# A gated delta-rule mixer: triangular inverses in three stages of two levels, and products of raw q and k

## The chip, the cores and the metric

One core of a Trainium2 chip runs the whole kernel. The metric is the device time in microseconds (us) of one execution; the times below are of three runs. Engines: PE is TensorE's matmul stream, PEld its weight loads, DVE is VectorE, ACT is ScalarE, POOL is GpSimd, SP is SyncE, which issues the DMAs.

## The reference

One step of a decoder layer for a prompt of 16 + 1024 tokens and 8 samples of 8 tokens: feed-forward, a mixer with two branches, feed-forward, final norm. The change lies in branch B, the gated delta rule over 8 heads of width 128:

```python
def l2norm(x):
    return x * lax.rsqrt(jnp.sum(x * x, axis=-1, keepdims=True) + L2_EPS)
...
    q = l2norm(q) * (GDN_DK ** -0.5)
    k = l2norm(k)
    beta = jax.nn.sigmoid(b_raw)
...
    a_kk = beta[..., :, None] * jnp.einsum('bnhid,bnhjd->bnhij', k, k) * dec_strict
    rhs = jnp.concatenate([beta[..., None] * v, (beta * jnp.exp(g))[..., None] * k], axis=-1)
    sol = lax.linalg.triangular_solve(a_kk, rhs, left_side=True, lower=True, unit_diagonal=True)
    u, w = sol[..., :dv], sol[..., dv:]
    a_qk = jnp.einsum('bnhid,bnhjd->bnhij', q, k) * dec_incl
...
        nu = u_c - w_c @ s
        o = qd_c @ s + aqk_c @ nu
        s = exp(gl_c) * s + kd_c.T @ nu
...
    o = rmsnorm(o, norm_g) * jax.nn.silu(zh)
```

## The kernel before

All tokens are one row of 1104 columns, features on the partitions. The kernel runs in stages: turning the inputs, feed-forward 1, the mixer (from about 860 to 2310 us), the merge of the branches, feed-forward 2, the output. In float32 the large products are made of three passes over a high and a low part of each operand (`three_passes`, L209 to L211), each a matmul with 368 moving columns.

The mixer first projects q, k and v for eight heads, with a short convolution on VectorE (`head_conv`, L1897). Then come 16 full **turns** and two odd ones for the last 80 tokens. A turn u handles 128 tokens of four heads (group g = u mod 2) and carries, as filler on TensorE, 36 pieces of dense projections (z, the gates, branch A), six matmuls each. `turn_order` (L884) writes one list of steps, and every engine walks that list in order, doing its part of each step; a step in `NEXT_STEPS` (L939) is done for the turn that follows. Two turns make one pass of a hardware loop.

The steps of a turn: `kk` and `qk` (products of k with k and with q), `kt` (transposes of k and v to tokens on the partitions; L1523, L1526), `zero` (T0 transposes the first level of the masked matrix, L1529, and starts the inverse). Then the inverse of the 128 x 128 unit triangle is doubled in six levels: `Y` (L1533) multiplies the masked level with the transposed inverse, ScalarE copies it, `X` (L1543) multiplies that with the half of the inverse's columns that changes, VectorE subtracts (L1888), `T` (L1537) transposes the result, ScalarE copies it (L1736). Between them: `ks` (L1568, k with the state), and for the next turn the sums `dec`, `eg`, `sq`, `sk` (all L1503, 512 columns wide), where sq and sk sum the squares of q and k, from which ScalarE makes the norms by Ln and Exp (L1723, L1727) and VectorE scales q and k in place (`scale`, L1865, L1868). At the end `nu`, `o` and `ds` (L1548, L1574, L1580), `os` (L1552: sum of the squares of the output), and `out` (Ln, Exp and the scaled output; L1739, L1741, L1894). `evict` empties a projection's bank: VectorE first, and in group-1 turns ScalarE with Silu or Sigmoid (L1780). `split` makes the high and low parts of the next weight (L812 on ScalarE, L817 on GpSimd). `conv` is a step of branch A's convolution on VectorE. GpSimd masks levels (L1386), the decay and others. SP loads q, k and v of the next turn at the start of a turn, in group-0 turns only after the y and gate stores of the turn before.

Turn 0 is prepared in the last pass of `head_conv`: four sums on TensorE between projections (L1654), and the scaling of q and k at j = 2 (L1918).

Of the kernel before, what the change touches and what calls it, by code (L numbers as in the profile page):

```python
# [36 lines left out]
EPS = 1e-6  # L37
SC_T = 3
# [790 lines left out]
class Events:  # L829


    def __init__(self, s, label):
# [14 lines left out]
        self.rooted = s.sem(label + "rooted")  # L847
        self.y_ready = s.sem(label + "y_ready")
# [3 lines left out]
class HeadGroup:  # L852
# [31 lines left out]
def turn_order():  # L884
# [17 lines left out]
    order.append(("lu", 0))  # L902
    dense(1)
    order.append(("qk", 0))
    order.append(("kt", 0))
    dense(1)
    order.append(("zero", 0))
    order.append(("square", 0))
    dense(2)
    for k in range(1, LEVELS):  # L910
        order.append(("Y", k))
        if k == 1:
            order.append(("ks", 0))
# [12 lines left out]
        dense(1 if k > 4 else 2)  # L926
# [12 lines left out]
NEXT_STEPS = ("load", "lu", "square", "dec", "eg", "sq", "sk", "mask", "scale")  # L939
# [84 lines left out]
for _name, _width in (("upto", P), ("upto_tail", TAIL), ("after", P), ("after_tail", TAIL), ("level", LEVELS * P),  # L1024
# [6 lines left out]
def delta_constants():  # L1031
# [7 lines left out]
    def put(name, a):  # L1039
# [7 lines left out]
                                 for k in range(LEVELS)], 1))  # L1047
# [4 lines left out]
def mixer(nc, base, h_hi, h_lo, slots, ahead, w_a, raw_at, x_at, x, rstd, gains, ones, ident, eps_col, w_in, sc_taps, gc_taps, sc_hist, gc_hist, sc_tail, gc_tail,  # L1052
# [8 lines left out]
    with ExitStack() as ctx:  # L1061
# [50 lines left out]
        state = m.sb("state", [P, H, P])  # L1112

# [7 lines left out]
        N = Units(s, "n", [(name, 0) for name in ("dec", "eg", "sq", "sk")], [n_bank])  # L1121
        names = ["kk", "qk", "kt", "vt", "T0"]
        for k in range(1, LEVELS):
            names += [f"Y{k}"] + (["ks"] if k == 1 else []) + [f"X{k}"] + ([f"T{k}"] if k < LEVELS - 1 else [])
# [27 lines left out]
        full = [HeadGroup(P, g, LEVELS, N, A, full_on) for g in range(2)]  # L1152
        for g, d in enumerate(full):
            d.q, d.k, d.v, d.eg = q[g], k_n[g], v[g], eg[g]
            d.qk_loaded, d.v_loaded = s.sem(f"qk_loaded{g}"), s.sem(f"v_loaded{g}")
            d.sq, d.lu, d.dec, d.bdec, d.bmat, d.bk, d.aqk, d.w_inv, d.y_lev = sq, lu, dec, bdec, bmat, bk, aqk, w_inv, y_lev
            d.kdec, d.resid, d.x_inv, d.nu, d.o, d.o_sq = kdec, v_tok, x_inv, nu, o, o_sq
            d.upto, d.after = const("upto"), const("after")
# [7 lines left out]
        tails = [HeadGroup(TAIL, g, TAIL_LEVELS, N, O, full_on) for g in range(2)]  # L1166
# [7 lines left out]
        for g, d in enumerate(tails):  # L1174
# [3 lines left out]
            d.sq, d.bk = odd_view(sq[:, :, :, :], P, 2, HG, TAIL), odd_view(bk[:, :, :, :], TAIL, 2, HG, TAIL)  # L1178
# [197 lines left out]
        def _(pool):  # L1376
# [1090 lines left out]
```

## Time and profile before

| | |
|---|---|
| median of three runs | 3411.95 us |
| lowest and highest | 3410.54 and 3413.16 us |
| the profiled execution | 3409.4 us |
| its span, first to last instruction | 3407.6 us |
| PE busy | 3300.6 us, 97% |
| VectorE, ScalarE, GpSimd busy | 39%, 30%, 26% |
| granted clock of TensorE, mean over the span | 0.983 |
| first to last full turn's start | 1162.45 to 2107.20 us |

How to read it: engines run beside each other, so shares don't add up. A busy PE is not PE at its peak, as matmuls are pipelined and each lasts longer than the distance to the next; what a matmul costs is read start to start in the timeline. A line of waits names what an engine sat idle for, and what ended the idle time.

### The profile page before, as it was taken

To read this page: it belongs to the slowest core of one execution; us is meant where nothing else is said; L and a number is where in the kernel's file an instruction comes from. 1 tells how busy PE (TensorE), PEld (TensorE's weight loads), DVE (VectorE), ACT (ScalarE), POOL (GpSimd) and SP (SyncE) were. 2 spreads that over 40 slices of the span, in tenths; PEclk is the share of its full clock that TensorE was granted. 3 is DMA by queue.
4 is the path that set the end of the run, shared out by engine and by line. 5 is a ranking of instruction groups with operands and counts; after the bars stand their busy time and mean duration, and the time that the engine had idled before them with its cause. 6 is when DMAs were issued, how large, how long until landed. Compare 5 with 4: busy or idle time off the path is not lost. (4 is left out here: it accounts for less than half of the span.)

```text
span 3407.6 us, 51601 instructions
## 1 busy us (share of the span) xinstructions
PE 3300.6 (97%) x20286; PEld 3228.4 (95%) x20286; DVE 1343.8 (39%) x2193; ACT 1018.3 (30%) x1412; POOL 891.1 (26%) x506
## 2 busy tenths in 40 slices
PE   8999999998999999999999999898999999999998
PEld 8999999998999899999999999878999999999997
DVE  4333333334677633333333333344224333333333
ACT  5111111113322354554544544412123111111113
POOL 2121111123222333333323323221143122211212
PEclk9999999999999999999999999898999999999998
DMA  4111111112233212212112112438212111111101
GB/s 134 44 41 48 46 44 43 37 39 72 70 95 100 87 52 63 65 52 70 59 51 68 57 51 72 141 105 291 78 41 72 38 49 43 43 43 43 40 28 53
DMA packets 275570, 227.04 MB, mean 67 GB/s; under 512 B 12170, under 2 KB 251914, under 8 KB 275440
## 3 DMA queue, kind: packets, MB, share of 16 engines
q1 hardware_dynamic: 275140, 225.08, 21.8%
q8 instruction: 84, 1.38, 0.2%
q10 hardware_dynamic: 324, 0.41, 0.0%
q14 instruction: 22, 0.18, 0.0%
HBM read 172.92 MB, written 52.54 MB: 66 GB/s over the span
## 5 line engine op out<-in xcount | busy, mean ns | idle before, releaser
L209 PE MATMUL ffn_bank<-ffn_h_hi,ffn_w_hi 128*128 128x368 f32 x2112 | 698.1, 331 | 6.8 <-DVE ffn_h_lo L618 6.8
L210 PE MATMUL ffn_bank<-ffn_h_lo,ffn_w_hi 128*128 128x368 f32 x2112 | 699.0, 331 | 0.0
L211 PE MATMUL ffn_bank<-ffn_h_hi,ffn_w_lo 128*128 128x368 f32 x2112 | 697.7, 330 | 0.0
L209 PE MATMUL mix_bank<-both_h_hi,mix_w_hi 128*128 128x368 f32 x1848 | 676.7, 366 | 10.8 <-issue 5.9
L408 POOL TENSOR_TENSOR ffn_w_lo<-g_w_raw,ffn_w_hi 128x1024 fp32r<-128x1024 f32 x130 | 310.9, 2401 | 1191.7 <-ACT ffn_w_hi L404 1191.6
L210 PE MATMUL mix_bank<-both_h_lo,mix_w_hi 128*128 128x368 f32 x1848 | 613.1, 332 | 0.0
L211 PE MATMUL mix_bank<-both_h_hi,mix_w_lo 128*128 128x368 f32 x1848 | 611.9, 331 | 0.0
L817 POOL TENSOR_TENSOR mix_w_lo<-g_w_raw,mix_w_hi 128x1024 fp32r<-128x1024 f32 x77 | 196.4, 2551 | 837.2 <-ACT mix_w_hi L812 837.2
L209 PEld LDWEIGHTS ffn_bank<-ffn_h_hi,ffn_w_hi 128*128 128x128 f32 x2112 | 398.2, 189 | 8.1 <-issue 8.0
L211 PEld LDWEIGHTS ffn_bank<-ffn_h_hi,ffn_w_lo 128*128 128x128 f32 x2112 | 398.0, 188 | 0.0
L210 PEld LDWEIGHTS ffn_bank<-ffn_h_lo,ffn_w_hi 128*128 128x128 f32 x2112 | 397.7, 188 | 0.1
L209 PEld LDWEIGHTS mix_bank<-both_h_hi,mix_w_hi 128*128 128x128 f32 x1848 | 351.5, 190 | 34.6 <-issue 26.1
L645 DVE SCALAR_TENSOR_TENSOR g_x<-ffn_bank,g_x 128x368 f32<-128x368 f32 x528 | 284.1, 541 | 225.7 <-PE ffn_bank L211 225.4
L210 PEld LDWEIGHTS mix_bank<-both_h_lo,mix_w_hi 128*128 128x128 f32 x1848 | 351.5, 190 | 20.8 <-issue 19.1
L211 PEld LDWEIGHTS mix_bank<-both_h_hi,mix_w_lo 128*128 128x128 f32 x1848 | 350.2, 189 | 0.0
L211 PE MATMUL ffn_bank<-ffn_mid_hi,ffn_w_lo 128*128 128x368 f32 x1056 | 349.3, 331 | 0.0
L210 PE MATMUL ffn_bank<-ffn_mid_lo,ffn_w_hi 128*128 128x368 f32 x1056 | 349.1, 331 | 0.0
L209 PE MATMUL ffn_bank<-ffn_mid_hi,ffn_w_hi 128*128 128x368 f32 x1056 | 348.8, 330 | 0.0
L404 ACT ACTIVATE ffn_w_hi<-g_w_raw 128x1024 fp32r<-128x1024 f32 x132 | 136.4, 1051 | 456.0 <-PE ffn_bank L211 444.9
L629 DVE TENSOR_TENSOR ffn_hid<-ffn_bank,g_rstd 128x368 f32<-128x368 f32 x132 | 71.1, 541 | 431.3 <-PE ffn_bank L211 431.3
L209 PEld LDWEIGHTS ffn_bank<-ffn_mid_hi,ffn_w_hi 128*128 128x128 f32 x1056 | 198.7, 188 | 0.7
L211 PEld LDWEIGHTS ffn_bank<-ffn_mid_hi,ffn_w_lo 128*128 128x128 f32 x1056 | 198.7, 188 | 0.0
(252 smaller groups left out, 4390.2 us busy)
## 6 DMA issues: line engine op xcount, KB each, us to landing
g_w_raw<-in_w_in SPq DMA_DIRECT2D x73, 512.0 KB, 5.6
g_w_raw<-in_ffn_w_gate SPq DMA_DIRECT2D x44, 512.0 KB, 3.9
g_w_raw<-in_ffn_w_up SPq DMA_DIRECT2D x44, 512.0 KB, 3.8
g_w_raw<-in_ffn_w_down SPq DMA_DIRECT2D x44, 512.0 KB, 3.6
scratch_qkv<-mix_out SPq DMA_DIRECT2D x24, 552.0 KB, 2.8
turn_kq<-scratch_qkv SPq DMA_DIRECT2D x32, 256.0 KB, 3.6
scratch_x<-g_x SPq DMA_DIRECT2D x8, 552.0 KB, 6.4
scratch_z<-turn_z_out SPq DMA_DIRECT2D x8, 552.0 KB, 2.8
```

The costliest lines, as they stand in the source:

```text
L209: pe.matmul(out, w_hi, x_hi, start=first, stop=False)
L210: pe.matmul(out, w_hi, x_lo, start=False, stop=False)
L211: return pe.matmul(out, w_lo, x_hi, start=False, stop=last)
L404: act.activation(self.hi[:, u, :, :], self.raw[:, u % self.RAW, :, :], ACT.Copy).then_inc(self.hi_done, 1)
L408: pool.tensor_tensor(self.lo[:, u, :, :], self.raw[:, u % self.RAW, :, :], self.hi[:, u, :, :].bitcast(F32), ALU.subtract).then_inc(self.l ...
L629: dve.tensor_tensor(hid[:, a, third(b)], bank[b][:, 0:TH], rstd[:, third(b)], ALU.mult).then_inc(bank_free[b], 1)
L645: return dve.scalar_tensor_tensor(x[:, c, third(b)], bank[n % 6][:, 0:TH], 0.5, x[:, c, third(b)], ALU.mult, ALU.add)
L817: pool.tensor_tensor(self.lo[:, k, :, :], self.raw[:, k, :, :], self.hi[:, k, :, :].bitcast(F32), ALU.subtract).then_inc(self.lo_done, 1)
```

## The change

In full turns (128 tokens) only; the two odd turns keep the old form.

- **The inverse** goes in three stages of two levels. A stage k is `E` (masked levels times the transposed inverse, copied by ScalarE), then three products `Za`, `Zb`, `Zc` with the same copied matrix, full width, each followed by a subtraction on VectorE (z = x - Za, z = x - Zb, x = x - Zc), and but for the last stage `T`. Four masks replace seven.
- **q and k stay raw.** The sums sq and sk, their Ln and Exp, and the scaling of q and k are gone. `k_tok` transposes the next turn's k (in place of kt's transposes), VectorE makes kdec from it, ScalarE sums its squares per token (four Squares with an accumulator), then Ln and two Exp of 128 x 4 numbers give the norm of k and `rate`, which VectorE multiplies with beta. v is multiplied with the norm when it is read from PSUM (step `vt`, now on VectorE, before a copy on ScalarE); `rate` takes beta's place in bdec and nu.
- **The norm of q** goes into the output's own norm: `q_sq` squares q on ScalarE, and at `os` VectorE adds it to the output's squares ahead of the sum on TensorE; the constant added under the root is changed accordingly.
- **Order**: `dec` moves to stage 1 behind Zb, `eg` to stage 2 behind E; the branch A steps `conv` 1 to 5 move, the last to behind Zc of stage 3. In the last full turn the odd turn's square, sq, sk and scale stand in these places.
- **The start**: k_tok, dec and eg between the projections; k_tok on VectorE at j = 0, no scaling at j = 2.

The diff, cut to its core:

```diff
@@ turn_order @@
     order.append(("kk", 0))
     order.append(("lu", 0))
+    order.append(("q_sq", 0))
     dense(1)
     order.append(("qk", 0))
-    order.append(("kt", 0))
+    order.append(("vt", 0))
     dense(1)
     order.append(("zero", 0))
-    order.append(("square", 0))
     dense(2)
-    for k in range(1, LEVELS):
-        order.append(("Y", k))
+    for k in range(1, STAGES + 1):
+        order.append(("E", k))
         if k == 1:
             order.append(("ks", 0))
-        if k <= 4:
-            order.append((("dec", "eg", "sq", "sk")[k - 1], 0))
-        dense(1)
-        order.append(("X", k))
-        dense(2 if k > 4 else 1)
-        order.append(("T", k))
-        if k == 2:
+            order.append(("k_tok", 0))
+        elif k == 2:
+            order.append(("eg", 0))
+        dense(2)
+        order.append(("Za", k))
+        if k == 1:
+            order.append(("rate", 0))
+        elif k == 2:
+            order.append(("conv", 2))
+        dense(2)
+        order.append(("Zb", k))
+        if k == 1:
+            order.append(("dec", 0))
+        elif k == 2:
             order.append(("mask", 0))
-        if k == 6:
-            order.append(("scale", 0))
-        if k < 6:
-            order.append(("conv", k))
-        dense(1 if k > 4 else 2)
+            order.append(("conv", 3))
+        dense(2)
+        order.append(("Zc", k))
+        order.append(("conv", (1, 4, 5)[k - 1]))
+        dense(1 if k < STAGES else 2)
+        if k < STAGES:
+            order.append(("T", k))
+            dense(1)
     order.append(("nu", 0))
@@ GpSimd @@
                 elif name == "qk":
...
+                    if d.n == P:
+                        pool.wait_ge(d.on.qsq_ready, h + 1)
...
+                elif name == "E" and k < STAGES:
+                    d.units.wait_done(pool, d.at(h), f"E{k}")
+                    mask_level(d, k + 1)
@@ TensorE @@
+                elif name == "k_tok":
+                    pe.wait_ge(d.qk_loaded, t * 32 + 32)
+                    d.norms.wait_bank(pe, u, "k_tok")
+                    for hd in range(HG):
+                        mm = pe.transpose(d.norms.ps("k_tok")[:, hd * P:(hd + 1) * P], d.k[:, hd, :], ident[:, :])
+                    mm.then_inc(d.norms.done, 1)
...
+                elif name in ("Za", "Zb", "Zc"):
+                    before, src = {"Za": (f"E{k}", d.x_inv), "Zb": (f"Za{k}", d.z), "Zc": (f"Zb{k}", d.z)}[name]
+                    U.wait_read(pe, u, before)
...
+                    per_head(d, h, f"{name}{k}", n, n, lambda out, hd: pe.matmul(out, d.y_lev[:, hd, :], src[:, hd, :], start=True, stop=True))
...
                 elif name == "os":
-                    pe.wait_ge(d.on.osq_ready, h + 1)
+                    if n == P:
+                        pe.wait_ge(d.on.osum_ready, h + 1)
+                    else:
+                        pe.wait_ge(d.on.osq_ready, h + 1)
...
-            sums_at = {(4, 2): "dec", (5, 0): "eg", (5, 1): "sq", (5, 2): "sk"}
+            sums_at = {(4, 2): "k_tok", (5, 0): "dec", (5, 1): "eg"}
@@ ScalarE @@
+                elif name == "q_sq":
+                    act.wait_ge(d.qk_loaded, t * 32 + 32)
+                    act.activation(d.q_sq, d.q[:, :, :], ACT.Square, scale=P * EPS ** 0.5).then_inc(d.on.qsq_ready, 1)
+                elif name == "k_tok":
...
+                    act.wait_ge(d.on.kdec_ready, h + 1)
+                    for hd in range(HG):
+                        ins = act.activation(d.dec[:, hd, :], d.ps("k_tok", P, P)[:, hd, :], ACT.Square, accum_out=d.k_sum[:, hd:hd + 1])
+                    ins.then_inc(d.norms.sem("k_tok"), 1)
+                    d.norms.wait_read(act, u, "k_tok")
+                    act.activation(d.k_log, d.k_sum, ACT.Ln, bias=eps_col).then_inc(d.on.k_logged, 1)
+                    act.wait_ge(d.on.k_logged, h + 1)
+                    act.activation(d.k_norm, d.k_log, ACT.Exp, scale=0.5)
+                    act.activation(d.rate, d.k_log, ACT.Exp, scale=-1.0).then_inc(d.on.k_rooted, 1)
...
-                elif name == "kt" and n == P:
-                    U.wait_done(act, u, "vt")
-                    act.copy(d.resid[:, :, :], d.ps("vt", P, P)).then_inc(U.sem("vt"), 1)
+                elif name == "E":
+                    U.wait_done(act, u, f"E{k}")
+                    act.copy(d.y_lev[:, :, :], d.ps(f"E{k}", n, n)).then_inc(U.sem(f"E{k}"), 1)
@@ VectorE @@
+                elif name == "k_tok":
+                    d.norms.wait_done(dve, u, "k_tok")
+                    dve.tensor_tensor(d.kdec[:, :, :], d.ps("k_tok", P, P), tok(d, 3, t, P), ALU.mult).then_inc(d.on.kdec_ready, 1)
+                elif name == "rate":
+                    dve.wait_ge(d.on.k_rooted, h + 1)
+                    dve.tensor_tensor(d.rate, d.rate, tok(d, 1, t, 1).rearrange("p h o -> p (h o)"), ALU.mult).then_inc(d.on.rate_ready, 1)
+                elif name == "vt":
+                    U.wait_done(dve, u, "vt")
+                    dve.wait_ge(d.on.k_rooted, h + 1)
+                    dve.tensor_tensor(d.resid[:, :, :], d.ps("vt", P, P), d.k_norm.unsqueeze(2).broadcast_to([P, HG, P]), ALU.mult) \
+                        .then_inc(U.sem("vt"), 1)
+                elif name == "os" and n == P:
+                    dve.wait_ge(d.on.osq_ready, h + 1)
+                    dve.wait_ge(d.on.qsq_ready, h + 1)
+                    dve.tensor_tensor(d.o_sq[:, :, :], d.o_sq[:, :, :], d.q_sq, ALU.add).then_inc(d.on.osum_ready, 1)
...
+                elif name in ("Za", "Zb"):
+                    U.wait_done(dve, u, f"{name}{k}")
+                    dve.tensor_tensor(d.z, d.x_inv[:, :, :], d.ps(f"{name}{k}", n, n), ALU.subtract).then_inc(U.sem(f"{name}{k}"), 1)
+                elif name == "Zc":
+                    U.wait_done(dve, u, f"Zc{k}")
+                    dve.tensor_tensor(d.x_inv[:, :, :], d.x_inv[:, :, :], d.ps(f"Zc{k}", n, n), ALU.subtract).then_inc(U.sem(f"Zc{k}"), 1)
...
-                    if scale_first and j == 2:
-                        shared(full[0], "scale", 0, 0, None, 0)
+                    if scale_first and j == 0:
+                        dve.wait_ge(prep_act, 4)
+                        shared(full[0], "k_tok", 0, 0, None, 0)
...
+                    if scale_first and j == 0:
+                        dve.wait_ge(prep, 2)
+                        shared(full[0], "rate", 0, 0, None, 0)
```

## Rows read from the trace of the kernel before

**Rows 1.** The page: busy time of each engine, its share of the span, instructions.
```profile
PE 3300.6 (97%) x20286; PEld 3228.4 (95%) x20286; DVE 1343.8 (39%) x2193; ACT 1018.3 (30%) x1412; POOL 891.1 (26%) x506
```

**Rows 2.** Waits of TensorE, 1174 to 2165: waiter, releaser, us, times, longest.
```profile
PE mix_a_bank L1533 <- issue: 10.2, 8, 1.3
PE mix_a_bank L1529 <- POOL turn_bk L1386: 6.5, 12, 1.3
PE mix_bank L209 <- issue: 5.9, 4, 1.9
```

**Rows 3.** Timeline, TensorE, turn 7: start, duration, line, out<-in, shapes, count.
```profile
1613.39 1.05 PE L1533 MATMUL mix_a_bank<-turn_w_inv,turn_bk 128*128 128x128 f32 x8
1614.28 1.06 PE L1568 MATMUL mix_a_bank<-turn_state,turn_kq 128*128 128x128 f32 x8
1615.18 1.02 PE L1503 MATMUL mix_n_bank<-turn_lu,mix_con 128*128 128x512 f32 x2
...
1616.21 0.33 PE L210 MATMUL mix_bank<-both_h_lo,mix_w_hi 128*128 128x368 f32 x1
...
1617.04 1.00 PE L1543 MATMUL mix_a_bank<-turn_x_inv,turn_y_lev 128*128 128x64 f32 x8
...
1618.10 0.32 PE L210 MATMUL mix_bank<-both_h_lo,mix_w_hi 128*128 128x368 f32 x1
...
1618.94 0.60 PE L1537 MATMUL mix_a_bank<-g_ident,turn_x_inv 128*128 128x128 f32 x4
...
1619.55 0.33 PE L210 MATMUL mix_bank<-both_h_lo,mix_w_hi 128*128 128x368 f32 x1
```

**Rows 4.** Timeline, ScalarE and TensorE, turn 7: T4's copy and Y5.
```profile
1643.46 0.57 ACT L1736 COPY turn_w_inv<-mix_a_bank 128x512 f32<-128x512 f32 x1
...
1644.13 1.13 PE L1533 MATMUL mix_a_bank<-turn_w_inv,turn_bk 128*128 128x128 f32 x8 [1.30 <-issue]
```

**Rows 5.** Timeline, ScalarE, VectorE and TensorE, turn 7 to 8: out to T0.
```profile
1666.89 1.04 ACT L812 ACTIVATE mix_w_hi<-g_w_raw 128x1024 fp32r<-128x1024 f32 x1
...
1671.98 0.75 DVE L1894 SCALAR_TENSOR_TENSOR turn_o<-turn_o,mix_g_norm,turn_o_sq 128x512 f32<-128x512 f32 x1 [5.54 <-ACT turn_o_sq L1741]
...
1674.84 0.65 PE L1529 MATMUL mix_a_bank<-g_ident,turn_bk 128*128 128x128 f32 x4 [0.32 <-POOL turn_bk L1386]
```

**Rows 6.** Timeline, ScalarE: a Square with accumulator; a table load and its function.
```profile
7.39 1.06 ACT L334 ACTIVATE tr_row_sq<-tr_rows 128x1024 f32<-128x1024 f32 x1
8.35 0.19 ACT L334 ACTIVATION_READ_ACCUMULATOR tr_row_sq<-tr_rows 128x1 f32 x1
...
1623.08 1.28 ACT L1719 ACT_TABLE_LOAD   x1
1624.37 0.60 ACT L1719 ACTIVATE turn_eg<-mix_n_bank 128x512 f32<-128x512 f32 x1
```

**Rows 7.** Timeline, VectorE and TensorE, turn 7: residual sum, X's update, state, os.
```profile
1616.22 1.50 DVE L2015 TENSOR_TENSOR turn_v_tok<-turn_v_tok,turn_nu 128x512 f32<-128x512 f32 x1
...
1625.18 0.42 DVE L1888 TENSOR_TENSOR turn_x_inv<-turn_x_inv,mix_a_bank 128x256 f32<-128x256 f32 x1 [0.30 <-PE mix_a_bank L1543]
...
1662.04 1.12 DVE L2020 SCALAR_TENSOR_TENSOR turn_state<-turn_state,turn_eg,mix_a_bank 128x128 f32<-128x128 f32 x4 [3.14 <-PE mix_a_bank L1580]
...
1663.85 1.02 PE L1552 MATMUL mix_a_bank<-turn_o_sq,g_ones 128*128 128x512 f32 x2
```

**Rows 8.** Turn 0's T0; last row a window: busy times, PEclk (0.57), DMA, GB/s.
```profile
1158.83 0.69 DVE L1865 SCALAR_TENSOR_TENSOR turn_kq<-turn_kq,turn_sq 128x512 f32<-128x512 f32 x1 [0.21 <-DVE mix_pre L1914]
1159.44 2.87 DVE L1868 TENSOR_TENSOR turn_kq<-turn_kq,turn_sq 128x512 f32<-128x512 f32 x1
...
1170.12 0.74 PE L1529 MATMUL mix_a_bank<-g_ident,turn_bk 128*128 128x128 f32 x4 [2.73 <-POOL turn_bk L1386]
...
1170.00:1174.00 4.00, 3.88 (x15) 3.89 (x16) 2.36 (x3) 0.99 (x2) 4.00 (x4) 0.57 0.46 150
```

**Rows 9.** Timeline, ScalarE, turn 8: the Squares wait for the next q and k.
```profile
1678.87 1.15 ACT L1710 ACTIVATE turn_sq<-turn_kq 128x512 f32<-128x512 f32 x2 [4.74 <-DMA turn_kq<-scratch_qkv]
```

More of the change, by code:

```diff
@@ L37 @@
 EPS = 1e-6
+L2_EPS = 1e-6
 SC_T = 3
@@ L938 @@
 TURN_ORDER = turn_order()
-NEXT_STEPS = ("load", "lu", "square", "dec", "eg", "sq", "sk", "mask", "scale")
+NEXT_STEPS = ("load", "lu", "k_tok", "rate", "square", "dec", "eg", "sq", "sk", "mask", "scale")
 WA = NQ + 3 * TURNS
@@ L950, in last_full_order @@
             order += [("dense", 35), ("evict", 8), ("ya_split", 0), ("os", 0), ("ya_split", 1)]
-        elif (name, k) in (("split", 2), ("dense", 35), ("evict", 8)):
+        elif (name, k) in (("split", 2), ("dense", 35), ("evict", 8), ("rate", 0)):
             pass
+        elif name == "k_tok":
+            order.append(("square", 0))
+        elif name == "Za" and k > 1:
+            order += [(name, k), (("sq", 0), ("scale", 0))[k - 2]]
+        elif (name, k) == ("Zb", 2):
+            order += [(name, k), ("sk", 0)]
         elif name == "out":
@@ L1023 @@
 _at = 0
-for _name, _width in (("upto", P), ("upto_tail", TAIL), ("after", P), ("after_tail", TAIL), ("level", LEVELS * P),
+for _name, _width in (("upto", P), ("upto_tail", TAIL), ("after", P), ("after_tail", TAIL), ("level", (TAIL_LEVELS + STAGES) * P),
                       ("segment", NSEG)):
@@ L1120, in mixer @@
         a_banks = [s.ps(f"a_bank{k}", [P, 512]) for k in range(4)]
[L1121 to L1124, printed above, removed]
+        N = Units(s, "n", [(name, 0) for name in ("k_tok", "dec", "eg")], [n_bank])
+        NO = Units(s, "no", [(name, 0) for name in ("dec", "eg", "sq", "sk")], [n_bank])
+        names = ["kk", "qk", "vt", "T0"]
+        for k in range(1, STAGES + 1):
+            names += [f"E{k}"] + (["ks"] if k == 1 else []) + [f"Za{k}", f"Zb{k}", f"Zc{k}"] + ([f"T{k}"] if k < STAGES else [])
         names += ["nu", "o", "ds", "os"]
@@ L1151, in mixer @@
         full_on = Events(s, "")
-        full = [HeadGroup(P, g, LEVELS, N, A, full_on) for g in range(2)]
+        full = [HeadGroup(P, g, MASKS, N, A, full_on) for g in range(2)]
         for g, d in enumerate(full):
@@ L1155, in mixer @@
             d.qk_loaded, d.v_loaded = s.sem(f"qk_loaded{g}"), s.sem(f"v_loaded{g}")
-            d.sq, d.lu, d.dec, d.bdec, d.bmat, d.bk, d.aqk, d.w_inv, d.y_lev = sq, lu, dec, bdec, bmat, bk, aqk, w_inv, y_lev
-            d.kdec, d.resid, d.x_inv, d.nu, d.o, d.o_sq = kdec, v_tok, x_inv, nu, o, o_sq
-            d.upto, d.after = const("upto"), const("after")
+            d.lu, d.dec, d.bdec, d.bmat, d.bk, d.aqk, d.w_inv, d.y_lev = lu, dec, bdec, bmat, bk, aqk, w_inv, y_lev
+            d.q_sq, d.kdec = sq[:, 0, :, :], kdec if g else sq[:, 1, :, :]
+            d.resid, d.x_inv, d.nu, d.o, d.o_sq = v_tok, x_inv, nu, o, o_sq
+            d.k_sum, d.k_log, d.k_norm, d.rate = [k_stat[:, r, g, :] for r in range(4)]
+            d.upto, d.after, d.z = const("upto"), const("after"), bk[:, 0, :, :]
         def odd_view(buf, rows, *shape):
@@ L1196, in tok, with rate_of @@
             return a.broadcast_to([d.n, HG, width])
+        def rate_of(d, h, t, width):
+            if d.n != P:
+                return tok(d, 1, t, width)
+            return d.rate.unsqueeze(2).broadcast_to([P, HG, width])
         def over_heads(a, d):
@@ L1529, in shared @@
                     per_head(d, h, "T0", n, n, lambda out, hd: pe.transpose(out, d.bk[:, 0, hd, :], ident[0:n, 0:n]))
+                elif name == "E":
+                    pe.wait_ge(d.on.bk_ready, d.masks(h) + (k + 1))
+                    U.wait_read(pe, u, f"T{k - 1}")
+                    per_head(d, h, f"E{k}", n, n, lambda out, hd: pe.matmul(out, d.bk[:, 1, hd, :], d.w_inv[:, hd, :], start=True, stop=True))
+                elif name in ("Za", "Zb", "Zc"):
+                    before, src = {"Za": (f"E{k}", d.x_inv), "Zb": (f"Za{k}", d.z), "Zc": (f"Zb{k}", d.z)}[name]
+                    U.wait_read(pe, u, before)
+                    if name == "Za" and k == 1:
+                        pe.wait_ge(d.on.x_started, h + 1)
+                    per_head(d, h, f"{name}{k}", n, n, lambda out, hd: pe.matmul(out, d.y_lev[:, hd, :], src[:, hd, :], start=True, stop=True))
                 elif name == "Y":
@@ L1588, in odd_step @@
                 U, g, u = d.units, d.g, d.at(h)
-                if name in ("kk", "kt") and g == 0:
+                if name == "dec" and g == 0:
+                    pe.wait_ge(N.free[0], TURNS * N.bank_per[0] + 1)
+                    pe.sem_inc(NO.free[0], 1)
+                elif name in ("kk", "kt") and g == 0:
                     for b in ((0, 1, 3) if name == "kk" else (2,)):
@@ L1761, in _ @@
             ins.then_inc(prep_act, 1)
-            shared(full[0], "square", 0, 0, None, 0)
+            shared(full[0], "k_tok", 0, 0, None, 0)
             w.split_hi(act, H - 1, 3, 4)
```

100 lines of the change are left out of this document (60 added, 40 removed).

## Prediction

> **What bounds the kernel now.** First the page's busy times: TensorE is busy for 97% of the span and no other engine for more than 39% [rows 1]. Then the waits of TensorE alone, from the first to the last full turn: 22.6 us of idle in some 990, at three places [rows 2]. So a turn costs what TensorE issues in it, plus its few waits, and an edit is worth the TensorE time that it adds or removes. I therefore read the timeline of one turn for prices, start to start, because the busy times of pipelined matmuls overlap. u counts turns from 0; g is the head group; odd u are group-1 turns.
>
> **Prices on TensorE** [rows 3]. From 1616.21 to 1617.04 five dense matmuls are issued: 0.166 us each, so a dense piece of six is 1.0. A block of four products 128 wide (Y) takes 1614.28 - 1613.39 = 0.89. A 512-wide sum (dec) takes 1616.21 - 1615.18 - 0.17 = 0.86. A block of four half-wide products (X) takes 1618.10 - 1617.04 - 0.17 = 0.89. A block of four transposes (T) takes 1619.55 - 1618.94 - 0.17 = 0.44.
>
> A half-wide X costs as much as a full Y; this decides the change. Six Y and six X give way to three E and nine Z, twelve blocks for twelve, at 0.89 each: zero. The Trainium skill, "TensorE: Matmul & The Clock Gate", section "Back-to-back issue gap", prices an isolated product by the columns that stream, and by that estimate X would be worth half of Y and the new inverse six half blocks dearer, about 2.7 us a turn, which would eat the whole gain. Its section "LDWEIGHTS" prices the load by the 128 stationary columns alone, and the trace agrees with that one: 0.89 for both widths.
>
> **Part by part, full turns.** T drops from five to two: -3 x 0.44 = -1.33. The sums sq and sk go: -2 x 0.86 = -1.73. The transposes kt go from between qk and vt, and the same block comes back as k_tok after ks. The dense work is the same 36 pieces.
>
> I count from T0 to the last dense piece, and from there to the next T0, since the second stretch is ruled by another chain. The first loses 1.33 + 1.73 - 0.44 = 2.61 per turn: 15 x 2.61 = **-39.2**. Turn 15 has no k_tok, and the tail keeps its sq and sk: **-1.3**.
>
> The second stretch [rows 5]: when the last dense piece is done, ScalarE splits a weight (1666.89), then Ln and Exp with a table load each, VectorE scales o (1671.98) and makes bmat, GpSimd masks it, and only then may T0 start (1674.84). TensorE waits there in 12 turns [rows 2]. No member of this chain changes, so the removed kt only lengthens that wait: **0**. In u = 2, 4 and 6 a wait at the loop's start comes first and T0 isn't late; there 0.44 is saved: **-1.3**.
>
> **The wait that goes.** Y5 of group-1 turns waits: T4's copy on ScalarE starts only at 1643.46, behind Ln, Exp and table loads of sq and sk, and Y5 starts at 1644.13 [rows 4]. The sq/sk chain is gone, and with it the eight waits of 1.3: **-10.2** [rows 2].
>
> **The wait that comes.** k_tok puts a new ScalarE chain behind E1: four Squares with sums, Ln, two Exp. A Square with its accumulator read moves on every (8.35 - 7.39) + 0.1 for 1024 columns; at 128 columns I estimate 0.31. A table load is followed by its function after 1.29 [rows 6]. In the clock of u = 7 with E1 at 1613.39, blocks and covers of 2.0 give k_tok 1615.17, Za1 1617.6, Zb1 1620.5, Zc1 (with dec) 1624.25, T1 1626.1, E2 1627.6. VectorE: the residual sum starts at 1616.22; it took 1.50 beside two GpSimd masks, of which one is left, so I take 0.69, a 128 x 512 operation undisturbed [rows 8]; then kdec, 0.69 again, done 1617.6 [rows 7]. ScalarE: Squares to 1618.9, Ln 1620.4, Exp 1622.0. In a group-1 turn there follow, each with a load, Silu (1623.8), Exp of dec (1625.7), Silu (1627.4), then the split (0.95) and T1's copy (0.58, [rows 4]): 1629.0. E2 starts at 1629.1 instead of 1627.6, a wait of 1.5. Bounds: none if the Squares and small functions overlap; 2.3 if the residual sum still takes 1.50. Seven turns (in u = 15 only the tail's Squares stand there): 7 x 1.5 = **+10.5**. Group-0 turns have no Silu on ScalarE and T1's copy is free in time.
>
> The last rule to weigh is one on those loads. The Trainium skill, "ScalarE: Activation LUTs", section "What ACT_TABLE_LOAD costs", counts a drain of 1.38 us on top of each load of 1.28; by that estimate five loads would make the wait 6.9 longer. The trace does not agree: the load at 1623.08 lasts 1.28 and the Exp starts at 1624.37.
>
> **Smaller terms.** os now waits for VectorE, which adds q's squares after the state update: 1662.04 + 1.12 + 0.69 + about 0.2 for two hand-overs (an estimate) = 1664.05 against 1663.85 [rows 7]: 16 x 0.2 = **+3.2** (0 to 8). Zc's update is 0.69 where X's was 0.42 (L1888), with the same single dense piece of cover before T. That was enough for 0.42; the 0.27 more could all be slack or all be a wait, and as VectorE sat idle ahead of X's update I take it as nearly slack, 0.025 at each of 32 hand-overs: **+0.8** (0 to 9). k_tok needs q and k of the next turn: in u = 8 they have landed at 1678.87 [rows 9], and k_tok comes at T0 + 0.44 + 2.0 + 2 x 0.89, 1679.1: **+0.5** (0 to 7).
>
> Hidden: `rate` on VectorE waits for ScalarE until 1622.1, and behind it are queued Zb1's update and an eviction; Zb1 is done at 1621.4, its update at 1622.9, and Zc1 wants it at 1624.25. Without that cover each late microsecond of ScalarE would stop TensorE in all turns. The Za and Zb updates (0.69) lie under two pieces (2.0). GpSimd makes four masks, not seven, and was idle anyway; its new waits for `rate` come a stage later. vt's scaling takes kdec's old place on VectorE. SP's store of y_a moves behind Zc3, with three loads behind it in u = 15; some 8 us are left before ScalarE casts them. q's Square runs in ScalarE's idle time ahead of its first eviction.
>
> **The start.** Ahead of turn 0, sums fall from 4 x 0.86 to 2 x 0.86 + 0.44 (-1.3), and the scaling of q and k leaves VectorE's last convolution. It took 0.69 and 2.87; the 2.87 started beside a GpSimd split, which will now hold up the convolution, so I count 2 x 0.69. T0 of turn 0, at 1170.12, waits for that queue [rows 8]: **-2.7**. TensorE idles 2.73 before it and runs at a clock of 0.57 in the 4 us behind, at 1.2 GHz for most of them; I leave that as it is.
>
> **Sum.** -39.2 - 1.3 - 1.3 - 10.2 + 10.5 + 3.2 + 0.8 + 0.5 - 2.7 = -39.7. The profiled execution took 3409.4 (its span and 1.8 around it), which gives 3369.7. The median of the three runs is 2.55 above that execution: **3372**.
>
> **Rivals.** (a) ScalarE's chain is longer, E2 waits about 3 us, and a half clock follows, as behind the 2.73 of turn 0 [rows 8]; the waits of 1.9 at the loop's start drew none. The clock of 0.57 over 4 us costs 4 x 0.43 = 1.7; price 7 x (1.5 + 1.7) = 22, so 3394. Against it: my sum has the wait at 1.5. Chance 0.12.
> (b) It ends slower. Place: ScalarE's queue ahead of T1's copy in group-1 turns. If each of its five table switches costs another 1.28 there, E2 waits 7.9, and with the half clock 7 x (6.4 + 1.7) = 57 comes on top: 3429. It decides from a wait of 1.5 + 39.7 / 7 = 7.2 on, or less with the half clock. Against it: the function follows its load at once [rows 6]. Chance 0.04. This is how the drain that the Trainium skill states would act here.
> (c) The q and k loads reach k_tok late in group-0 turns, since SP sends them behind the y and gate stores: 1 us late in eight turns is 8, so 3380. For it: only 0.2 of slack. Chance 0.08.
> (d) The inverse costs more than before, because a half-wide product is worth half of a wide one after all: six blocks dearer by 0.45 lose 2.7 a turn, 16 x 2.7 = 43, and the time stays, at 3415. Against it: both take 0.89 [rows 3]. Chance 0.03. By columns alone the Trainium skill's isolated gap would have it so.
>
> **Chances.** Forecast 0.73, the rivals as given. The forecast's own bounds are E2's wait (-10 to +6) and the small terms (-5 to +10, of which not all will be at their ends): 3357 to 3388. To leave out no more than 2 in 10 the range takes in (c) and (a): 3357 to 3394. Runs of this kernel tell 0.2% (6.8 us) from no change: faster 0.92, the same 0.04 ((d) and a bit), slower 0.04 ((b)).
>
> **What would show it.** After the change, turns of T0 to T0 near 59 to 62 us; Z blocks at 0.89 each; TensorE's waits now at E2 in odd turns (near 1.5, released by ScalarE's copy), at T0 (0.4 longer than before) and a short one at os. Wrong would be: waits at Za, Zb or T in every turn; a granted clock below 1.00 in the turns; k_tok waiting for a DMA.

## The result, and the profile after

The changed kernel takes 3371.6 us (median of four runs, 3370.9 to 3373.9) against 3412.4 for the kernel before beside it: a ratio of 0.9882, 95% interval 0.9865 to 0.99. 3372 was forecast. The profiled execution took 3370.85, its span is 3369.1. The page's busy line answers to [rows 1]:

```profile
PE 3254.8 (97%) x20030; PEld 3193.3 (95%) x20030; DVE 1354.7 (40%) x2258; ACT 913.1 (27%) x1379; POOL 820.7 (24%) x458
```

TensorE is the bound as before, with 45.8 us less of busy time. Its waits in the same stretch as [rows 2] (what it waited for, the releaser, us, times, longest):

```profile
PE mix_a_bank L1579 <- POOL turn_bk L1422: 23.6, 16, 5.9
PE mix_a_bank L1583 <- issue: 8.3, 7, 1.2
PE mix_a_bank L1615 <- DVE turn_o_sq L1963: 4.1, 1, 4.1
PE mix_a_bank L1593 <- issue: 0.6, 1, 0.6
```

L1583 is E, L1579 is T0, L1615 is os, L1593 is Y in the first odd turn. The eight waits of Y5 and the four at the loop's start are gone; seven at E2 have come; T0 now waits in every turn. The chain that makes E2 late, in the timeline of ScalarE and TensorE, turn 7 (start, duration, line, out<-in, shapes; in brackets the idle time before it):

```profile
1597.10 1.28 ACT L1788 ACT_TABLE_LOAD   x1
...
1598.71 1.28 ACT L1790 ACT_TABLE_LOAD   x1
...
1600.33 1.28 ACT L1859 ACT_TABLE_LOAD   x1
...
1602.14 1.28 ACT L1797 ACT_TABLE_LOAD   x1
...
1604.05 1.28 ACT L1859 ACT_TABLE_LOAD   x1
...
1605.76 1.04 ACT L814 ACTIVATE mix_w_hi<-g_w_raw 128x1024 fp32r<-128x1024 f32 x1
1606.71 0.56 ACT L1817 COPY turn_w_inv<-mix_a_bank 128x512 f32<-128x512 f32 x1
...
1607.37 1.13 PE L1583 MATMUL mix_a_bank<-turn_w_inv,turn_bk 128*128 128x128 f32 x8 [1.21 <-issue]
```

From the load behind the four Squares on, ScalarE is never idle until T1's copy (L1817): five table loads take 6.4 of these 9.6 us. And os, on VectorE and TensorE, in the same turn:

```profile
1637.73 1.12 DVE L2127 SCALAR_TENSOR_TENSOR turn_state<-turn_state,turn_eg,mix_a_bank 128x128 f32<-128x128 f32 x4 [3.14 <-PE mix_a_bank L1642]
1639.07 0.69 DVE L1963 TENSOR_TENSOR turn_o_sq<-turn_o_sq,turn_sq 128x512 f32<-128x512 f32 x1 [0.22 <-DVE turn_state L2127]
...
1639.82 1.12 PE L1615 MATMUL mix_a_bank<-turn_o_sq,g_ones 128*128 128x512 f32 x2
...
2126.91 1.12 PE L1615 MATMUL mix_a_bank<-turn_o_sq,g_ones 128*128 128x512 f32 x2 [4.12 <-DVE turn_o_sq L1963]
```

os starts 2.09 us after the state update does, where it started 1.81 after it in [rows 7]; the last row is turn 15, whose add stands behind the first half of a split of y_a on VectorE.

In the table, **A** is the time from T0's start to the start of the last matmul of the turn's last dense piece, **B** from there to the next T0, both as means of turns 2 to 14 (even) and 1 to 13 (odd); **stage** is from T0 of turn 0 to T0 of turn 16. All are differences of start times in the traces. The experiments of the next section stand in it too; b names start from the kernel before, e names from the changed kernel.

| kernel | ratio to before (95%) | stage | A even | A odd | B even | B odd |
|---|---|---|---|---|---|---|
| before | 1 | 1010.0 | 53.11 | 54.65 | 8.33 | 9.50 |
| changed | 0.9882 (0.9865 to 0.9900) | 972.6 | 50.94 | 52.34 | 8.31 | 9.27 |
| b2_xwide | 1.0001 (0.9991 to 1.0010) | 1011.2 | 53.11 | 54.67 | 8.33 | 9.64 |
| b3_inverse | 0.9901 (0.9884 to 0.9917) | 975.5 | 51.83 | 51.81 | 8.33 | 9.28 |
| b1_out | 0.9974 (0.9964 to 0.9983) | 1000.3 | 53.13 | 54.59 | 7.85 | 8.69 |
| e1_tcopy | 0.9858 (0.9842 to 0.9875) | 963.7 | 50.95 | 50.99 | 8.32 | 9.27 |
| e2_os | 0.9865 (0.9848 to 0.9881) | 966.2 | 50.54 | 51.97 | 8.32 | 9.27 |
| e3_out | 0.9848 (0.9832 to 0.9865) | 961.6 | 50.92 | 52.29 | 7.43 | 8.60 |
| e5_chain | 1.0011 (1.0001 to 1.0020) | 1012.1 | 50.95 | 57.77 | 8.32 | 9.28 |
| e7_tback | 0.9957 (0.9940 to 0.9973) | 996.2 | 52.77 | 53.22 | 8.31 | 9.27 |
| e4_all | 0.9799 (0.9783 to 0.9816) | 944.6 | 50.55 | 50.55 | 7.42 | 8.60 |
| e6_split | 0.9782 (0.9765 to 0.9798) | 937.6 | 50.50 | 50.56 | 7.42 | 7.42 |

The stage gives -37.4 of the profiled pair's -38.6; the start gives -4.1 and the rest of the kernel takes 2.9 back. Those two scatter: T0 of turn 0 falls at 1170.1 to 1171.0 in before, b1 and b2, and at 1166.0 to 1168.5 in the changed kernel and e1 to e7; what follows T0 of turn 16 takes 1227.5 to 1230.4 in the first three and 1230.0 to 1233.0 in the others. So I judge steps by the stage.

### The profile page after: what moved, and what is told of

Same layout as the page of the kernel before. It is cut to its first block and busy times, and to the rows that moved or that the text cites. A ratio compares the mean times of both kernels' runs of the same rounds, so it can differ in the third digit from the quotient of the medians.

```text
span 3369.1 us, 50801 instructions
## 1 busy us (share of the span) xinstructions
PE 3254.8 (97%) x20030; PEld 3193.3 (95%) x20030; DVE 1354.7 (40%) x2258; ACT 913.1 (27%) x1379; POOL 820.7 (24%) x458
## 5 line engine op out<-in xcount | busy, mean ns | idle before, releaser
L211 PE MATMUL mix_bank<-both_h_hi,mix_w_hi 128*128 128x368 f32 x1848 | 661.3, 358 | 5.1 <-DVE mix_pre L2014 3.2
```

The costliest lines, as they stand in the source:

```text
L211: pe.matmul(out, w_hi, x_hi, start=first, stop=False)
```

## The experiments

### Is a half-wide product as dear as a wide one? (b2_xwide)

```diff
-per_head(d, h, f"X{k}", n, n // 2, ... pe.matmul(halved(out, k), d.y_lev[:, hd, :], halves(d.x_inv[:, hd, :], k, 1), ...
+per_head(d, h, f"X{k}", n, n, ... pe.matmul(out, d.y_lev[:, hd, :], d.x_inv[:, hd, :], ...
```

> The kernel before, with the products X of full turns made over all 128 columns instead of the 64 that change; VectorE still subtracts the same half. Theory: four products 64 or 128 columns wide take 0.89 us alike, so the turns and the time stay: 3411 to 3414. Rival (d) of the prediction: a half-wide product is worth half of a wide one; then each X block grows by 0.45 us and the time by 16 x 6 x 0.45 = 43 us, to 3455.

Measured: 3409.8 us against 3409.8. The X block, now 128 wide, and the second dense matmul after it (timeline of TensorE, turn 7):

```profile
1617.05 1.05 PE L1544 MATMUL mix_a_bank<-turn_x_inv,turn_y_lev 128*128 128x128 f32 x8
...
1618.11 0.32 PE L210 MATMUL mix_bank<-both_h_lo,mix_w_hi 128*128 128x368 f32 x1
```

1618.11 - 1617.05 - 0.17 = 0.89, what the half-wide block takes in [rows 3]; A is the same to 0.02. Rival (d) is out, and with it, for products of this kind, the isolated gap by streaming columns of the Trainium skill ("TensorE: Matmul & The Clock Gate", "Back-to-back issue gap"). A Z block of the changed kernel takes as much, 1599.81 - 1598.92 = 0.89 (timeline of TensorE, turn 7; the second row is dec, which follows it):

```profile
1598.92 1.05 PE L1589 MATMUL mix_a_bank<-turn_bk,turn_y_lev 128*128 128x128 f32 x8
1599.81 1.02 PE L1546 MATMUL mix_n_bank<-turn_lu,mix_con 128*128 128x512 f32 x2
```

Twelve wide blocks for six wide and six half-wide ones are a swap at no cost.

### The inverse alone (b3_inverse)

The edit in short, not in the kernel's own lines:

```diff
-for k in range(1, LEVELS): Y, X and T of one level
+for k in range(1, STAGES + 1): E, Za, Zb, Zc and T of two levels
 # kept: square, sq, sk, scale, kt; placed at
+dec: E1    eg: Zb1    sq: E2    sk: Za2    mask: Zb2    scale: Zb3
```

> The kernel before with the inverse alone changed to three stages of two levels; q and k are still scaled, with the sums sq and sk, their logarithm and exponentials, kt, and the norms as before. dec stands at E1, eg at Zb1, sq at E2, sk at Za2, the mask at Zb2, scale at Zb3. Theory: three transposes of 0.44 us a turn go, 16 x 1.33 = 21.3, and with them the wait of 1.3 us at Y5 in eight turns, 10.2, as the steps with sq and sk no longer stand right ahead of a copy that TensorE waits for: about 3380. The part of the change that has to do with norms is then worth only 3380 - 3371.6 = 8 us, though it removes 1.73 - 0.44 us of TensorE work a turn, because it brings the wait at E2. Rival: the wait at Y5 comes back as one at E2 or E3, since ScalarE still has sq's and sk's logarithms and table loads: then 3390. The waits of 5.9 us at the loop's start in turns 2 to 8, which went with the whole change, tell in passing which part removed them.

Measured: 3375.0 against 3409.8, -34.8. TensorE's waits, in the stretch of the table above:

```profile
PE mix_a_bank L1547 <- POOL turn_bk L1401: 17.8, 16, 6.5
PE mix_a_bank L1541 <- ACT turn_o_sq L1768: 3.3, 1, 3.3
PE mix_a_bank L1561 <- issue: 0.6, 1, 0.6
```

No wait at any E, and none at the loop's start. A falls by 1.28 in even turns (three T blocks, forecast 1.33) and by 2.84 in odd ones (with the wait at Y5). So the inverse carries most of the gain: 34.5 of the stage's 37.4, of which 1.6 come from the waits at the loop's start that are gone with it. The norm part is worth the other 2.9 only, and the two parities show why: against b3 the whole change saves 0.89 in an even turn (1.73 - 0.44 of blocks, less 0.40 at os) but **costs 0.53 in an odd one**, where the wait at E2 (1.34) comes on top.

### What E2 waits for (e1_tcopy, e5_chain)

```diff
 ScalarE, step T:
-elif name == "T" and k < d.levels - 1:
+elif name == "T" and k < d.levels - 1 and not (n == P and d.g == 1 and k == 1):
 VectorE:
+elif name == "T" and n == P and d.g == 1 and k == 1:
+    U.wait_done(dve, u, "T1")
+    dve.tensor_copy(d.w_inv[:, :, :], d.ps("T1", n, n)).then_inc(U.sem("T1"), 1)
```

> The changed kernel, with one move: in turns of group 1 the copy of T1 to the buffer that E2 reads runs on VectorE instead of ScalarE. In the changed kernel TensorE waits seven times at E2 in these turns, 1.18 us idle each (8.3 us together), which costs 1.34 us from step to step. Theory: the wait is for ScalarE's queue, where the four Squares, the logarithm, two exponentials and two table loads of the next turn's norms stand ahead of the T1 copy. Then the idle time at E2 goes to about 0 and the time falls by 7 x 1.34 = 9.4 us from 3371.6 to about 3362. Rival: E2 waits for GpSimd's level mask or for another releaser, and the T1 copy only comes last by a little: then E2 still waits over 0.8 us and the time stays at 3371 to 3373.

Measured: 3364.3, and -8.9 in the stage. No wait at E (L1583) is left:

```profile
PE mix_a_bank L1579 <- POOL turn_bk L1422: 24.0, 16, 6.3
PE mix_a_bank L1615 <- DVE turn_o_sq L1963: 4.1, 1, 4.1
PE mix_a_bank L1593 <- issue: 0.6, 1, 0.6
```

A in odd turns falls by 1.35 to the even turns' value. E2 waited for ScalarE's queue and for nothing else. The opposite experiment makes that queue longer:

```diff
 ScalarE, step k_tok, behind rate:
+if d.g == 0:
+    act.activation(k_more[:, 0, :], d.k_sum, ACT.Ln, bias=eps_col)
+    act.activation(k_more[:, 1, :], d.k_sum, ACT.Exp, scale=-1e-6)
```

> The changed kernel with one more logarithm and exponential of 128 x 4 numbers, each with its table load, behind the rate's exponential in group-1 turns (and once ahead of turn 0); their results are not used. ScalarE's chain ahead of T1's copy grows by 2 x (1.28 + 0.2) = 3.0 us. Theory: the wait at E2 grows by as much, from 1.2 to 4.2 us, and nothing else: 7 x 3.0 = 21 us, to 3393. Rival (a) of the prediction: an idle time of that length also draws a half clock behind it, 1.7 us each: 12 more, to 3405, with a granted clock below 1.00 behind each E2. Rival (b): a table switch costs 1.28 us beyond its load: 7 x 2 x 1.28 = 18 more, to 3411, and the wait at E2 would be near 6.8.

The chain stands in group-1 turns, which prepare a turn of group 0. Measured: 3412.7; the whole gain of the change is gone, 39.5 of it in the stage. By the time alone rival (b), 3411, would fit better than (a), 3405; the wait at E2 decides between them:

```profile
PE mix_a_bank L1584 <- issue: 30.0, 7, 4.3
```

the added work on ScalarE and E2 behind it:

```profile
1618.17 1.28 ACT L1794 ACT_TABLE_LOAD   x1
1619.46 0.30 ACT L1794 ACTIVATE turn_k_more<-turn_k_stat,g_eps 128x4 f32<-128x4 f32 x1
1619.77 1.28 ACT L1795 ACT_TABLE_LOAD   x1
1621.06 0.20 ACT L1795 ACTIVATE turn_k_more<-turn_k_stat 128x4 f32<-128x4 f32 x1
...
1628.32 2.04 PE L1584 MATMUL mix_a_bank<-turn_w_inv,turn_bk 128*128 128x128 f32 x8 [4.29 <-issue]
```

and two windows behind it (busy us of PE, PEld, DVE, ACT and POOL with counts, then the granted clock, DMA share, GB/s):

```profile
1628.00:1632.00 4.00, 3.68 (x11) 2.68 (x12) 0.00 (x0) 1.80 (x3) 3.73 (x3) 0.50 0.30 124
1632.00:1636.00 4.00, 4.00 (x25) 4.00 (x24) 0.97 (x2) 2.68 (x4) 1.99 (x2) 0.85 0.00 0
```

The wait grows by 3.1, from 1.2 to 4.3: two loads of 1.28 with their functions, no more. That excludes rival (b), which puts the wait near 6.8; the drain of 1.38 that the Trainium skill ("ScalarE: Activation LUTs", "What ACT_TABLE_LOAD costs") adds to each load would have made it 4.3 + 2 x 1.38, 7.1, by an estimate from that page, and the trace does not agree. But an odd turn's A grows by 5.43, not by 3.1: behind the 4.3 us of idle TensorE runs at 0.50, that is at 1.2 GHz, and E2's block of four products takes 1.83, to the sum that starts behind it at 1630.15, instead of 0.97 in the changed kernel. That is rival (a) of the prediction in its mechanism; its price of 1.7 a turn for the half clock is short, 5.43 - 3.1 = 2.3 is measured. In the changed kernel itself the 1.2 at E2 leaves the clock at 1.00.

### What os waits for (e2_os)

```diff
-step os:  dve.tensor_tensor(d.o_sq, d.o_sq, d.q_sq, ALU.add)       # behind the state update
+step o:   dve.tensor_tensor(d.o_sq, d.o_sq, d.q_sq, ALU.add)       # ahead of it
```

> The changed kernel, with one move: VectorE adds q's squares to the output's squares in step o, ahead of the state's update (1.12 us), instead of at step os behind it. In the changed kernel TensorE's os step is 1.248 us long from start to start against 0.853 before, in every turn, and in the last turn it waits 4.12 us for that add behind VectorE's other work. Theory: os waits for VectorE's queue, so the step goes back to 0.85 us and the time falls by 15 x 0.395 = 6 us, and by up to 4 more for the last turn, to 3362 to 3366. Rival: the add's own length sets it and not its place in the queue: then the os step stays above 1.15 us and the time at 3371 to 3373. A second rival: the step shortens but the wait for T0 at the turn's end grows by as much, because the chain from os over the output's root to T0 starts earlier but ends as late: then under 2 us of it are left.

Measured: 3366.1, and -6.5 in the stage. VectorE now adds first, and the state update follows it without a gap:

```profile
1637.59 0.69 DVE L2122 TENSOR_TENSOR turn_o_sq<-turn_o_sq,turn_sq 128x512 f32<-128x512 f32 x1 [2.95 <-ACT turn_o_sq L1867]
1638.20 1.12 DVE L2126 SCALAR_TENSOR_TENSOR turn_state<-turn_state,turn_eg,mix_a_bank 128x128 f32<-128x128 f32 x4
...
1639.59 1.02 PE L1615 MATMUL mix_a_bank<-turn_o_sq,g_ones 128*128 128x512 f32 x2
```

A falls by 0.40 and 0.37, and B doesn't grow: the second rival of this run is out too. In turn 15 the wait of 4.1 goes, but only 0.9 of it comes back, since that turn still waits for its T0.

### What T0 waits for (e3_out, b1_out)

```diff
 turn_order:
     order.append(("os", 0))
+    order.append(("out", 0))
     dense(1)
-    order.append(("out", 0))
```

> The changed kernel, with one move: each turn's out step (ScalarE's logarithm and exponential of the output's norm, VectorE's product) is put right behind os, ahead of the last dense piece with its eviction and weight split. In the changed kernel TensorE waits for T0's mask in every turn, 27.1 us in 17 waits, about 0.73 us idle where the next turn is of group 1 and 1.70 where it is of group 0. Theory: the chain that ends in T0 runs eviction or split, then out's table loads and functions, then the next kk's product on VectorE; with out earlier the waits go, 7 x 1.7 + 8 x 0.73 = 18 us, to about 3353. Rival: what comes last in that chain is the kk product and GpSimd's mask by themselves, 2.3 us of mask after kk: then the waits stay and the time is 3369 to 3373.

Measured: 3360.8, and -11.0 in the stage where 18 was expected. Even turns do what the theory says: B falls by 0.88 and no wait is left. Odd ones give 0.67 and keep a wait of 1.04. The timeline at the end of turn 7 names the next in line:

```profile
1638.83 1.28 ACT L1859 ACT_TABLE_LOAD   x1
1640.15 0.51 ACT L1859 ACTIVATE turn_gate_out<-turn_gate_out 128x368 f32<-128x368 f32 x1
1640.56 1.04 ACT L814 ACTIVATE mix_w_hi<-g_w_raw 128x1024 fp32r<-128x1024 f32 x1
...
1641.08 0.69 DVE L1967 TENSOR_TENSOR turn_bmat<-mix_a_bank,turn_bdec 128x512 f32<-128x512 f32 x1 [0.97 <-PE mix_a_bank L1569]
...
1641.69 2.39 POOL L819 TENSOR_TENSOR mix_w_lo<-g_w_raw,mix_w_hi 128x1024 fp32r<-128x1024 f32 x1 [19.55 <-ACT mix_w_hi L814]
1644.03 2.51 POOL L1422 TENSOR_TENSOR turn_bk<-turn_bmat,mix_con 128x512 f32<-128x512 f32 x2
...
1645.43 0.65 PE L1579 MATMUL mix_a_bank<-g_ident,turn_bk 128*128 128x128 f32 x4 [1.04 <-POOL turn_bk L1422]
```

bmat is done at 1641.8, but GpSimd is in the low part of the weight until 1644.0, because ScalarE split that weight only behind an eviction with a table load. Neither theory nor rival had named it. The same move in the kernel before:

> The kernel before, with one move: out is put right behind os, as in the run of the changed kernel that gained 11.0 us between T0 of turn 0 and T0 of turn 16. It asks what the block kt (0.44 us of transposes a turn) was worth where the chain from out to T0 sets the end of a turn. Theory: kt stood in the shadow of that chain, so without the chain's wait it shows again. Then from the last dense piece to T0 an even turn takes 7.43 + 0.44 = 7.87 us here, against 7.43 with the same move in the changed kernel and 8.33 before the move; an odd one takes 8.60, where GpSimd's weight split ahead of the mask ends last in both. The time falls by 8 x 0.46 + 4 x 0.68 and by 0 to 2 more in turns 1, 3 and 5, 6 to 9 us, to 3403 to 3406. Rival: kt cost nothing even there, and an even turn takes 7.43 here too: then 8 x 0.9 + 4 x 0.68 = 10 us and more, to under 3402.

Measured: 3401.3 against 3409.8, -8.5. The difference is within the theory's 6 to 9. The time itself is below its 3403 and would fit the rival, because the kernel before ran faster beside it than the 3411.95 that both started from, so the stretch decides: B of an even turn is 7.85, 0.42 above e3's 7.43. That is the block kt, which the change takes out of this stretch. So the prediction was right to count it at nothing there: in the kernel before and after, B is 8.33 and 8.31, and kt's 0.44 has become waiting time at T0 (0.31 us at turn 7 before, 0.74 after).

### The three moves together, and a fourth (e4_all, e6_split)

> The changed kernel with the three moves together (T1's copy of group 1 on VectorE, the output's sum of squares ahead of the state's update, out right behind os). Theory: they touch three different waits, so their gains add: 9.4 + 6 + 18 = 33 us, to about 3338. Rival: the moves share ScalarE's and VectorE's queues, and what one frees another takes: then the sum of the three single gains is missed by over 5 us.

Measured: 3343.5, and -28.1 in the stage; the single gains of the stage add to 8.9 + 6.5 + 11.0 = 26.4. They add, then; the 33 of the theory fails by e3's miss alone. The fourth move takes what e3 showed:

```diff
 turn_order, dense():
+            if n % 12 == 11:
+                order.append(("split", n // 12))
             if n % 4 == 3:
                 order.append(("evict", n // 4))
-            if n % 12 == 11:
-                order.append(("split", n // 12))
```

> The changed kernel with the three moves together, and a fourth: on ScalarE the split of the next weight stands ahead of the eviction that comes at the same dense piece. With out moved, T0 still waits about 1.0 us at the end of seven group-1 turns; there ScalarE loads a table and runs Sigmoid (1.28 + 0.5) before it starts the split at 1640.56, GpSimd makes the low part until 1644.03, and only behind that the masks for T0. Theory: with the split first, GpSimd is free about 1 us earlier and the seven waits go: 7 x 0.95 = 6.6 us, from 3343.5 to about 3337. Rival: GpSimd's two masks (2.5) with the kk product ahead of them end last by then, so that under 0.4 us a turn is gained: 3341 to 3344.

Measured: 3335.4, another 7.0 in the stage. B of odd turns is 7.42, that of even ones, with no wait left at T0 of turns 1 to 15. Turn 15 itself is 1.7 longer than in e4, 1.5 of it a new wait at its E2, whose cause no run here asked for. The low part starts at 1628.41, before ScalarE's eviction is done:

```profile
1628.41 2.40 POOL L819 TENSOR_TENSOR mix_w_lo<-g_w_raw,mix_w_hi 128x1024 fp32r<-128x1024 f32 x1 [18.29 <-ACT mix_w_hi L814]
1630.75 2.54 POOL L1422 TENSOR_TENSOR turn_bk<-turn_bmat,mix_con 128x512 f32<-128x512 f32 x2
```

This version beats both kernels: 0.9782 (0.9765 to 0.9798) of the time before, where the change alone gives 0.9882.

### The transposes back, and the waits at the loop's start (e7_tback)

```diff
 TensorE, step T:
+if n == P:
+    ...
+    for _ in range(2):
+        for hd in range(HG):
+            pe.transpose(U.ps(f"T{k}")[:, hd * P:(hd + 1) * P], d.x_inv[:, hd, :], ident[:, :])
 per_head(d, h, f"T{k}", ...)
```

> The changed kernel with the transposes of both T steps of a full turn issued three times over, to the same place: 16 transposes more a turn, 32 TensorE instructions more in one pass of the loop of two turns, which is TensorE's count in the kernel before. Theory for the price: a block of four costs 0.44 us, so a turn costs 4 x 0.44 = 1.76 more; in seven group-1 turns 0.88 of it fills the wait at E2 (idle there 1.18, then 0.3): 16 x 1.76 - 7 x 0.88 = 22 us, to 3394. On the idle time of 5.9 us at the loop's start in turns 2 to 8 of the kernel before, which is gone in the changed kernel: if the number of TensorE's instructions in the loop brings it, it is back and the time is 3398 to 3400; if not, there is no wait at the first dense matmul of those turns.

Measured: 3395.0, and +23.6 in the stage. A grows by 1.83 in even turns, 1.76 expected for four blocks, and by 0.88 in odd ones, with 0.3 left of the wait at E2:

```profile
PE mix_a_bank L1583 <- issue: 2.1, 7, 0.3
```

The loop has as many TensorE instructions as before, and no wait stands at its start. Their number is not what brought it.

## Why the prediction was right, point by point

- **TensorE's prices.** A block of four transposes costs 0.44: b3 finds 1.28 a turn for three, e7 1.83 for four. With sq and sk I counted -2.61: A of even turns fell by 2.17, which is 2.57 with os's 0.40 put back. The Z block is 0.89 as forecast (rows under b2). This term, -39.2, carried the forecast.
- **B counted at nothing.** Right, and for the reason given (b1 against e3). In turns 1, 3 and 5 I counted -1.3 for kt behind a wait at the loop's start that I took to stay; it is -1.6 (0.74 + 0.46 + 0.42), because that wait went and T0's took its place. b3, which keeps kt, gets the same 1.6 there (0.73 + 0.45 + 0.41). That number is near by luck.
- **Y5's wait, -10.2.** Gone, and b3 shows that the new inverse alone takes it away, even with sq and sk still on ScalarE. My reason, that "the sq/sk chain is gone", was not needed: in b3 those steps stand at E2 and Za2, with two dense pieces behind each product before the next copy, and nothing waits. The size was short too: I counted the idle time, 1.3, but b3's A falls by 2.84 - 1.28 = 1.56 more in odd turns than in even ones, some 12.5 in eight turns.
- **E2's wait, +10.5.** Mechanism and place right, size nearly so: 1.18 of idle, 1.35 by e1's difference, so 9.4. The chain ran as it was forecast, step by step: counted from E1, which is at 1591.79 now and was at 1613.39, the Squares were to start at 1596.0, Ln to end at 1598.8, dec's Exp at 1604.1, the copy at 1607.4 and E2 to start at 1607.5; measured are 1595.9, 1598.7, 1604.0, 1607.3 and 1607.4. The wait is 1.2 and not 1.5 because TensorE came to E2 0.16 later than forecast and E2 started 0.13 earlier.
- **os, +3.2: mis-sized.** It is 0.40 a turn, 6.3 in all, within the bounds of 0 to 8. The hand-over from the state update to the add is 0.22 by itself, where I had put 0.2 for both hand-overs: 0.28 of the 0.40 is the later start, and 0.10 is os itself, 1.12 in place of 1.02, which I counted at nothing.
- **Not foreseen: os of turn 15.** VectorE's add stands there behind a split of y_a, and TensorE idles 4.1 us. e2 takes it away and gets 0.9 back, so it is worth little, but I had looked at what is queued ahead of the add in the ordinary turn only.
- **Zc before T, +0.8, and k_tok's loads, +0.5: nothing.** No wait at Za, Zb, T or k_tok in any turn; rival (c) didn't happen. k_tok waits for its DMA only in e5 (1.5 us, once) and e7 (0.2, once).
- **The start, -2.7.** -4.1 in the profiled pair; the means of three and eight kernels (1170.4 and 1167.4) differ by 3.0. The idle time before T0 and the half clock behind it stayed, as assumed (3.5 us of idle where it was 2.7, a clock of 0.64 over four microseconds where it was 0.57).
- **Rival (a)** is a true mechanism that stayed off: e5 turns it on with 3 us more and pays 5.43 a turn. What kept it off is that ScalarE's queue was no longer than summed: the 1.2 of idle left the clock at 1.00. **Rivals (b) and (d)** are excluded by e5 and b2.

The sum came within a microsecond of the median, and that close it came by luck, since its errors cancel (forecast less measured). The stage as a whole is off by +0.4: E2 +1.1, os -3.1, Zc and k_tok +1.3, Y5 +2.3, turns 1, 3 and 5 +0.3, and the -1.5 that is left lies in the blocks and in turn 15. In the profiled pair the start adds +1.4 and the rest of the kernel -2.9. The 2.55 from the profiled execution to the median was 0.8 after the change, which adds +1.8.

What I didn't ask is what the change is made of. Of its two parts the inverse gives 34.5 of the stage's 37.4; the raw q and k give 2.9, since they pay for 1.29 of TensorE work a turn with ScalarE work in odd turns and an add on VectorE's way to os. With the T1 copy and the add moved (e1, e2) the norm part gives its 1.29 in every turn: A is 50.55 in e4 against 51.8 in b3.

## What to carry to other kernels

Price an edit per stretch between waits: a block removed where a chain on other engines ends last is worth nothing until that chain is shortened, and shortening it shows the next in line, which has to be read from the new trace. When a step gives TensorE work to an engine that TensorE also waits for, look in that engine's queue for the one operation that TensorE needs next, and move that operation to an idle engine or ahead of the new work; here one copy on another engine and three moves in the order gave 36 us more, nearly as much as the change itself. Before a wait is accepted as small, read the granted clock behind it, and behind the longer waits of the same trace.

## What the runs showed of the hardware

- **The clock after idle time.** In the changed kernel, 1.21 us idle at E2 and 1.70 at T0 of turn 2 leave the granted clock at 1.00; the 4.12 at os of turn 15 is followed by 0.63 over four microseconds, the 5.9 at T0 of turn 16 by 0.54, the 4.29 of e5 by 0.50 and 0.85. In a turn of 60 us, 3.1 us of added wait then cost 5.4. The windows behind E2 of turn 7, os of turn 15 and T0 of turn 16 (columns as under e5):

```profile
1607.00:1611.00 4.00, 3.63 (x21) 3.18 (x22) 0.54 (x1) 2.71 (x4) 4.00 (x3) 1.00 0.31 126
2127.00:2131.00 4.00, 4.00 (x23) 3.41 (x24) 1.27 (x2) 3.12 (x5) 0.00 (x0) 0.63 0.97 319
2138.00:2142.00 4.00, 3.36 (x15) 3.35 (x16) 2.75 (x3) 0.00 (x0) 4.00 (x4) 0.54 1.04 292
```

- **The waits at the loop's start go with instruction loads, in steps.** By the profile's page, the queue of instruction DMA moved 84 packets (1.38 MB) in the kernel before, with four waits at the first dense matmul of a pass, 0.7 to 1.9 us each; 66 (1.08 MB) in b1 with two waits; 102 (1.67 MB) in b2 with six; 47 in b3 and the changed kernel and 48 in e7 with none. Two waits go with some 18 packets each time. b1 and b2 hold practically the same instructions as the kernel before, so it isn't the program's length alone; e7 excludes the number of TensorE instructions. What decides whether a pass loads again was not settled.
